# TensorE's register work in the expert loop: the down slot is found behind the up product, the table word is loaded behind the down product

## What is computed

```python
def run_block(args):
    tok, wt, e = args
    xb = h[tok]
    hid = jax.nn.silu(xb @ w_gate[e]) * (xb @ w_up[e])
    return (hid @ w_down[e]) * wt[:, None]

y = lax.map(run_block, (slot_tok, slot_w, block_e))
return jax.ops.segment_sum(y.reshape(n_slots, d), slot_tok, num_segments=n_tok)
```

## Time and profile before

| | before |
|---|---|
| median of 3 runs | 1967.69 us |
| profiled execution, its own time | 1963.07 us |
| its span, first to last instruction | 1961.1 us |
| expert loop of layer 0, down products at 436.3 to 1042.4 us | 80 iterations |
| expert loop of layer 1, about 1434 to 1945 us | 48 iterations |

### The profile page before, as it was taken

The page is one execution under the profiler, slowest core; times in us unless marked ns, Lnnn a source line. Parts: engine busy times, 40 slices in busy tenths (PEclk is TensorE's granted clock), DMA queues, the critical chain, the costliest instruction groups (busy, mean ns, idle before and its releaser), DMA issues. The chain is left out here.

```text
span 1961.1 us, 40674 instructions
## 1 busy us (share of the span) xinstructions
PE 1741.1 (89%) x12455; PEld 736.7 (38%) x12456; DVE 848.6 (43%) x2899; ACT 599.6 (31%) x1239; POOL 243.2 (12%) x254
## 2 busy tenths in 40 slices
PE   5999689879989999899997599859799999999997
PEld 3445554423323333333332365535433333333332
DVE  2255583444544455545555426545423222222223
ACT  2142372223333333333332214234122223222222
POOL 0002300002222222222221000230000000000000
PEclk9999799989999999999998789969899999999999
DMA  9315620467999999999956752651589999999980
GB/s 337 103 68 196 232 66 1 193 230 286 407 413 413 396 371 410 413 392 359 371 196 247 284 171 99 226 205 34 204 341 414 391 373 414 415 413 414 414 328 21
DMA packets 155441, 552.02 MB, mean 281 GB/s; under 512 B 21000, under 2 KB 25836, under 8 KB 138488
## 3 DMA queue, kind: packets, MB, share of 16 engines
q1 hardware_dynamic: 132704, 507.10, 66.0%
q0 software_dynamic: 15984, 42.18, 5.8%
q10 hardware_dynamic: 6696, 1.98, 0.4%
HBM read 536.11 MB, written 24.25 MB: 286 GB/s over the span
## 5 line engine op out<-in xcount | busy, mean ns | idle before, releaser
L1327 PE MATMUL bank<-arena 128*32 128x512 f32 x4160 | 502.8, 601 | 22.2 <-issue 11.8
L1352 PE MATMUL bank<-arena 128*32 128x512 f32 x2048 | 251.4, 601 | 32.5 <-issue 31.5
L1327 PEld LDWEIGHTS bank<-arena 128*32 128x32 f32 x4160 | 112.3, 109 | 230.0 <-issue 218.1
L1872 DVE COPY arena<-arena 128x12 bf16 (+1 forms) x270 | 52.8, 196 | 255.7 <-issue 255.7
L978 ACT ACTIVATE arena<-bank 128x128 f32<-128x128 f32 x128 | 35.5, 277 | 384.4 <-PE bank L1393 372.8
L1927 DVE TENSOR_TENSOR arena<-arena,bank 64x512 f32<-64x512 f32 x130 | 88.5, 681 | 148.4 <-ACT arena L956 146.5
L987 ACT ACTIVATE arena<-bank 128x512 f32<-128x512 f32 x128 | 76.4, 597 | 228.0 <-PE bank L1352 228.0
L1072 PE MATMUL bank<-arena 128*128 128x512 f32 (+3 forms) x384 | 129.7, 494 | 3.7 <-DMA arena<-in_w_in 1.8
L730 POOL DMA_INDIRECT yrows<-arena x80 | 81.1, 1013 | 414.6 <-ACT arena L987 414.6
L1352 PEld LDWEIGHTS bank<-arena 128*32 128x32 f32 x2048 | 57.2, 109 | 159.5 <-issue 156.3
L1317 PEld LDWEIGHTS bank<-arena 128*128 128x128 f32 x528 | 74.2, 210 | 113.2 <-issue 111.5
(11 more groups left out here) (332 smaller groups left out, 1989.5 us busy)
## 6 DMA issues: line engine op xcount, KB each, us to landing
arena<-in_exp_w_gate SPq DMA_DIRECT2D x128, 1024.0 KB
arena<-in_exp_w_up SPq DMA_DIRECT2D x128, 1024.0 KB
arena<-in_exp_w_down SPq DMA_DIRECT2D x128, 1024.0 KB
arena<-in_w_ada SPq DMA_DIRECT2D x10, 3072.0 KB, 12.6
arena<-in_w_ada SPq DMA_DIRECT2D x8, 2048.0 KB, 13.0
arena<-in_w_in SPq DMA_DIRECT2D x8, 2048.0 KB, 9.2
arena<-yrows SPq DMA_DIRECT2D x16, 1024.0 KB, 18.3
arena<-in_w_out SPq DMA_DIRECT2D x4, 2048.0 KB, 10.0
```

The lines of the kernel that those rows point to most:

```text
L1327: ins = pe.matmul(bank[0][r:r + UNIT, :], XGT[:, c, hh, un, :], wv[un][:, :, hh, c, :], start=(c == 0), stop=(c == 3))
L1352: ins = pe.matmul(bank[2][r:r + UNIT, :], HIDT[:, c, UNIT * un:UNIT * un + UNIT], wv[un][:, c, cg * 512:(cg + 1) * 512], start=(c == 0), s ...
```

## The change

Two statements move on TensorE; no product, wait or transfer is added or removed. `experts_of(word_now)` and the move of `word` go from behind `turn_tokens` to directly behind the up product. The load of the table word for b + 2 goes from there to behind the down product, in front of `meta` and the loop's end.

```diff
                     in_slots(slot, step, up_and_turn)
+                    now, slot_now, step_now = experts_of(pe.snap(word_now))
+                    pe.reg_mov(word_now, word)
                     if last:
                         turn_tokens(0, b + 3)
                     else:
...
                             turn_tokens(1, half * 16 + 32)
-                    now, slot_now, step_now = experts_of(pe.snap(word_now))
-                    pe.reg_mov(word_now, word)
-                    pe.reg_mov(word_next, experts_word(b + 2))
                     if last:
                         pe.wait_ge(a_y, b + 2)
                         pe.wait_ge(v_ow, b + 1)
...
                     in_slots(slot_now, step_now, down_now)
+                    pe.reg_mov(word_next, experts_word(b + 2))
                     if not last:
                         meta(b + 5, b + 4)
```

## The result

The changed kernel takes **1995.73 us**, the median of 4 runs (1992.05 to 1999.05). The kernel before took 1969.59 us beside it (4 runs, 1965.31 to 1972.95). The ratio is 1.0136 with an interval of 1.0119 to 1.0154: 26 us, 1.4% slower. The forecast was 2002 us, in a range of 1977 to 2020. The profiled execution took 1992.05 us.

A forecast was written before the change was run, and what follows sets the result against it. Matmuls bound layer 1; layer 0 has idle time that TensorE's sequencer may cause, not DMA. Later up products 53 us, less 5, 3 and 11, give 34 us on the 1967.69 us median: 2002 us, range 1977 to 2020.

The forecast's parts named there:

- The place of the load: Layer 0, down product to up product: a serial sequencer stretch, at most 0.36 us early, takes 0.80 us more per iteration.
- 53 us of later up products: Layer 0: 73 iterations x 0.80 us = 58.4 us, less 5.2 us of spare time, delays the up products.
- The slot's search is free: Layer 0, ahead of the token turns: the single instruction moved there costs nothing, with hidden turns still ahead of the array.
- Layer 1 pays nothing: Layer 1's loop: with 0.80 us more the sequencer still comes 0.55 us early, so no loss.
- The down product's waits: Layer 0, 28.1 us idle ahead of the down product: 5 us gained at the load's old place, 11 us given back.
- late loads: Layer 0, ahead of the down product: in 17 of 79 iterations the sequencer came after the copy; removing this gains 5 us.
- late copies: Layer 0: ScalarE's copy starts 0.2 to 1.2 us late in 28 iterations, holding 21.6 us; half, 11 us, comes back.
- nearly all: Rival, layer 0: all 21.6 us of late copies come back, 9 us loss, 1977 us; chance of 6 to 17 us loss 0.14.
- nothing: Rival, layer 0: the late copies give nothing back, 48 us loss, 2016 us; chance of over 2012 us 0.2.
- The waits for weights: Layer 0, up weights: of 7.6 us of waits, 3 us come back because TensorE comes later and the weights don't.
- The reason against the queue rule: Layer 0, down product: TensorE's 64-instruction queue cannot hide the load, since the sequencer is held waiting for the copy.
- the queue covers the load: Rival, layer 0: the load fits behind down product and `meta`, leaving only the 5 us gain, 1963 us; chance of faster 0.07.

The follow-up runs named there:

- e2: Kernel before with only the load of the table word moved behind the down product, the slot's search left in place: 1990.79 us, ratio 1.013.
- e4: Changed kernel with its load behind the down product made twice: 2062.68 us, ratio 1.0518 to the kernel before.
- e3: Kernel before with both the slot's search and the load moved directly behind the up product: 1957.07 us, ratio 0.9966.
- e11: Kernel before, unchanged, profiled again beside the third group of experiments: 1972.43 us.
- e12: Changed kernel, unchanged, profiled again right after the unchanged kernel before: 1993.13 us.
- e1: Kernel before with only the slot's search moved behind the up product, the load left in place: 1965.1 us, ratio 1.0005.
- e9: Kernel before with search and load behind the up product and the wait for the copy of hidden values behind the branches: 1959.14 us, ratio 0.9961.
- e6: Changed kernel with the wait for the copy of hidden values moved behind the branches, directly ahead of the down matmuls: 1983.72 us, ratio 1.0107 to the kernel before.
- e10: Changed kernel with the copy's wait behind the branches and the load between the down product's 8th and 9th matmuls: 1970.56 us, ratio 1.0002 to the kernel before.
- e8: Kernel before with search and load behind the up product, the copy's wait behind the branches, and GpSimd's gather held until the hidden turns: 1964.31 us, ratio 1.0.

## Why the prediction was right, and where its sizes were off

**The place of the load: right.** The serial stretch from the down product's branch to L1335 had 0.36 us to spare at best, and the load was put into it. e2 shows that the load alone makes the loss, e4 that a second one adds 0.72 us in each iteration, e3 that the same load is free behind the up product.

**53 us of later up products: right.** Measured +57.3 us between the two first profiles, +55.9 us in the pair e11 and e12, and +53.4 us from e1 to e2.

**The slot's search is free: right** (e1, ratio 1.0005). **Layer 1 pays nothing: right**, but with less to spare than forecast: the 0.55 us was read from an iteration with the most cover, and the median left is 0.34 us.

**The down product's waits: right in direction and near in size.** The prediction gave 5 us for the late loads and 11 for half of the late copies, 16 in all; measured were 18.7 and 16.9. Taken apart by iteration, those in which the sequencer came late went from 5.6 to 0.6 us of idle time (5.7 to 0.6 in the pair), and the others from 23.1 to 8.9 (20.3 to 8.0). The late loads come from the landing of the gathered rows. Copies that start over 0.1 us behind the turns' end were 36 in the profile of before and 31 after, 33 and 27 in the pair; over 0.2 us they were 34 before, where the prediction counted 28. The whole distance from the turns' end to the copy summed to 30.6 us before and 16.7 after, and to 27.7 and 14.9 in the pair. So about half came back, as in the sum, and in these profiles the rivals "nearly all" and "nothing" are both out. That the 11 us came out near is luck: the term was a guess halfway between two mechanisms, and neither was shown. Nor does the total hang on it. In e1 and e2 there is no late copy to give anything back. In e1 the sequencer comes late in 38 iterations, with 13.6 us of idle time, the wait falls by 12.7 us from e1 to e2, and the ratio is the same (1.013).

**The waits for weights: mis-sized, and the sentence behind it too strong.** The prediction said that "DMA is not what holds it", and took 3 us from the 7.6 us of waits. All of them went: 7.6 us, and 8.5 in the pair. I had read the DMA share of the whole loop, 0.91. Its mid-part alone tells more. The first row is of the kernel before, the second of the changed one:

```profile
480.00:1000.00 520.00, 476.41 (x4244) 165.42 (x4236) 259.34 (x1096) 170.69 (x344) 138.65 (x137) 1.00 0.99 394
```

```profile
480.00:1000.00 520.00, 457.40 (x4096) 158.80 (x4092) 249.53 (x1056) 163.68 (x330) 134.33 (x132) 1.00 0.96 382
```

The kernel before ran its mid-loop at a DMA share of 0.99, with a loop 11 to 13 us longer than those of e3 and e9, the shortest. A wait added to the array in such a loop comes out smaller than itself, since waits for weights and the stretches of low clock behind them go; one removed comes out smaller too, since they grow (e3). By the first two profiles the sum reads 57.3 - 18.7 - 7.6 - 3.4 = 27.6 us for the stretch, where the prediction had 53 - 16 - 3 = 34: 4.3 us more ahead of the up product, 2.7 and 4.6 us more given back by the down product and the weights, and 3.4 us that no wait names.

**The reason against the queue rule: right in its outcome, incomplete in its cause.** The rival "the queue covers the load" was out, since the sequencer never gets past the down product before its first matmul starts (79 of 79 iterations in e6), and not only because it is held at the wait for the copy (e6, e10).

## What to carry to other kernels

Before you move register work behind a product, ask for the distance that the sequencer can have there: here it was the one product behind it, 1.9 us plus 0.2, and the stretch to the next product's last register instruction already filled 1.7 of them. The place that cost nothing here is behind the longest product (2.78 us) and ahead of the next thing that the sequencer must wait for. Read the DMA share over the steady part of a loop, not the whole, before you say that transfers do not hold it: here each us taken off the sequencer's waits came out as less than one. And compare profiles of one chip: the late copies, which come and go with it, came with 10 us more of waits ahead of the down product (e11 against e1).

## What the runs showed of the hardware

**How far the sequencer runs ahead of the array.** At the down product of before, after and e6 it never goes on sooner than 0.02 us behind the start of the first of the product's 16 matmuls, each with its weight load. In layer 1 of before a register instruction behind a full down product comes at 1528.97, the product at 1528.95; and L1438, which stands behind the 8 matmuls of L1306 and 8 of L1310, comes at 1530.83, against 1530.80 for the first of L1306. With 8 it ran ahead (e10). But the limit is not 16 matmuls everywhere: behind the up product 22 had still to start at L1451 in e6 (721.1), and 22 at the branch out of that product in all 71 iterations of before in which it can be read. The Trainium skill ("Advanced Engine Details and Errata", Engine Queue Depths) gives 64 for TensorE, "complicated with tiling". With their weight loads 22 matmuls are 44, which fits under it; at the down product the sequencer is held with 32, which the number alone does not explain. What the limit counts stays open.

**The token turns' wait for a semaphore holds the sequencer.** The next register instruction runs 0.05 us (0.28 us with one more branch between) after the gathered rows have landed, in 29 of 80 iterations, and in none sooner. Register work behind these turns is not hidden by them.

**What register work costs.** One load of a word into a register records 297 to 1005 ns, 308 in the median; with its address, its bounds check and the gaps it made 0.72 us in e4. A branch of layer 0's loop that does not have to wait records 63 to 233 ns, the one out of a product's body 169.

**The clock and the waits.** In the profile of before the up product at 559.18 had waited 1.79 us for weights; the granted clock is 0.50 from 560.2 to 563.6 us, and the product took 4.39 us instead of 2.78. In e11 a wait of 4.52 us came with 5.25 us.

**Still open: the late copies.** In nearly every second iteration ScalarE's copy of the turned values starts 0.1 to 1.2 us after the turns end, with nothing else for it to do, in the profiles of before, after, e9, e10, e11 and e12. In those of e1 to e8 there is none: the longest distance is 0.04 us. In the twelve experiments they go with the chip on which a group ran, and not with the program: e2 and e12 differ only in the place of the slot's search, which e1 shows to be free. The loop with them is 2.5 to 2.8 us longer (before and e11 against e1); where they are missing, the sequencer is late more often and the waits for weights are longer (11.9 us in e1 against 7.6). In the late cases the copy starts mostly 1.4 to 1.7 us, or some 0.75 us, after GpSimd's gather instruction starts, but no run that has them tried the gather elsewhere, and their cause was not settled.
